# Second block's attention: VectorE scales head h-1 before it masks head h, instead of after

## The reference

```
h = rms_norm_2(x, g_pre_mix)
q, k, v = split_heads(h, w_qkv)              # 16 heads of 64
sc = q @ k.T / 8 + bias[head]                # causal by chunks of 64; 256 queries, 256 keys
p = softmax(sc)                              # exp(sc - max) / sum
m = merge_heads(p @ v) @ w_o
x = x + rms_norm_2(m, g_post_mix)
x = x + rms_norm_2(swiglu(rms_norm_2(x, g_pre_ffn), w_gate, w_up, w_down), g_post_ffn)
```

## Time and profile before

| | us |
|---|---|
| median of three runs | 775.57 (774.2 to 777.39) |
| the profiled execution | 774.49, of which the span of instructions 772.7 |
| TensorE busy in the span | 734.9 (95%) |
| VectorE, ScalarE busy | 418.9 (54%), 338.0 (44%) |
| second block's attention, first mask to last values | 488.4 to 571.3 |
| granted TensorE clock, mean | 0.992 |

### The profile page before, as it was taken

One profiled execution on the slowest core, in us unless ns is written; L12 is line 12 of the kernel. 1 busy time (PEld: TensorE's weight loads), 2 busy tenths in 40 slices (PEclk: granted clock), 3 DMA queues, 4 the chain that ended last, 5 costly groups with the idle time before them and its releaser, 6 DMA issues.

```text
span 772.7 us, 12515 instructions
## 1 busy us (share of the span) xinstructions
PE 734.9 (95%) x5170; PEld 606.1 (78%) x5170; DVE 418.9 (54%) x738; ACT 338.0 (44%) x604; POOL 32.2 (4%) x64
## 2 busy tenths in 40 slices
PE   8999999999999999999877789999999999999997
PEld 8898888888788866666555559999878888888885
DVE  5667756667667421111010117666668777777675
ACT  5966565554444421111010128465656444344443
POOL 2700000000000000000000001000001000000001
PEclk9999999999999999999999999999999999999999
DMA  8953557347988999999999999953334454545101
GB/s 343 416 212 119 207 219 286 117 170 278 366 313 339 362 391 419 422 420 419 421 421 421 412 419 355 419 174 130 145 109 164 174 208 164 205 176 197 77 1 55
DMA packets 33018, 206.07 MB, mean 267 GB/s; under 512 B 3904, under 2 KB 4288, under 8 KB 11200
## 3 DMA queue, kind: packets, MB, share of 16 engines
q1 hardware_dynamic: 32960, 205.25, 68.2%
HBM read 204.18 MB, written 1.05 MB: 266 GB/s over the span
## 4 chain that ended last, share of the span: by engine, by line
PE 77%; DMA 12%; ACT 3%; SPq 3%; DVE 3%; issue 1%; POOL 0%; DVEq 0%; POOLq 0%; ACTq 0%
PE ps L697 41%; PE ps L767 10%; PE ps L770 5%; PE ps L1096 5%; DMA big<-in_w_gate_e 3%; DMA ext<-in_w_up_e 3%; DMA X<-in_w_down_e 3%; PE ps L1020 2%; PE ps L1117 2%; SPq L504 2%; PE ps L1127 1%; DVE wl L1821 1%; DMA big<-in_rel_ext 1%; ACT wh L1406 1%; SPq L530 1%
## 5 line engine op out<-in xcount | busy, mean ns | idle before, releaser
L1821 DVE TENSOR_TENSOR wl<-raw,wh 128x1024 fp32r<-128x1024 f32 (+3 forms) x181 | 213.2, 1195 | 132.4 <-ACT wh L1406 131.2
L1406 ACT CAST wh<-raw 128x1024 fp32r<-128x1024 f32 (+3 forms) x181 | 181.8, 1024 | 71.5 <-PE ps L697 47.6
L697 PE MATMUL ps<-wh,fra 128*128 128x512 f32 (+3 forms) x636 | 179.2, 367 | 0.5 <-DVE gb L2030 0.5
L697 PEld LDWEIGHTS ps<-wh,fra 128*128 128x128 f32 x636 | 112.9, 189 | 18.2 <-issue 1.0
L697 PE MATMUL ps<-wl,fra 128*128 128x512 f32 (+3 forms) x318 | 115.1, 362 | 0.0
L767 PE MATMUL ps<-fra,wh 128*128 128x512 f32 x352 | 110.7, 396 | 0.7 <-DVE fra L1832 0.7
L770 PEld LDWEIGHTS ps<-fra,wl 128*128 128x128 f32 x352 | 66.1, 188 | 15.5
L697 PE MATMUL ps<-wh,frb 128*128 128x512 f32 x240 | 74.3, 391 | 0.0
L770 PE MATMUL ps<-fra,wl 128*128 128x256 f32 x352 | 69.2, 278 | 0.0
L697 PE MATMUL ps<-fra,wh 128*128 128x256 f32 x368 | 68.0, 286 | 0.1
L697 PEld LDWEIGHTS ps<-wl,fra 128*128 128x128 f32 x318 | 59.9, 188 | 9.0
(11 more groups left out here) (291 smaller groups left out, 1009.7 us busy)
## 6 DMA issues: line engine op xcount, KB each, us to landing
raw<-in_dense SPq DMA_DIRECT2D x79, 1024.0 KB, 5.4
ext<-in_w_down_e SPq DMA_DIRECT2D x20, 1024.0 KB, 18.3
raw<-in_w_gate_e SPq DMA_DIRECT2D x17, 1024.0 KB, 23.4
ext<-in_w_up_e SPq DMA_DIRECT2D x14, 1024.0 KB, 21.1
big<-in_w_up_e SPq DMA_DIRECT2D x8, 1024.0 KB, 18.1
big<-in_w_gate_e SPq DMA_DIRECT2D x7, 1024.0 KB, 27.0
raw<-in_dense SPq DMA_DIRECT2D x13, 512.0 KB, 5.7
raw<-in_w_up_e SPq DMA_DIRECT2D x6, 1024.0 KB, 21.0
```

What stands on the lines that cost most here:

```text
L697: t = e.matmul(o, a, w, start=first and n == 0, stop=final and n == 2, skip_group_check=not check)
L1406: e.copy(halves(q)[0], piece_view(q)).then_inc(*up("wh", q))
L1821: e.tensor_tensor(l, piece_view(q), h.bitcast(F), ALU.subtract).then_inc(*up("wl", q))
```

## The change

In `attention` of VectorE a flag `late` is added. Where it is set, `soften(step)` is called behind the reciprocal and scaling of head step-1 and not ahead of it. Only the second block's attention sets it.

```diff
-        def attention(name, heads, soften, norm, finish):
+        def attention(name, heads, soften, norm, finish, late=False):
             for step in range(heads + 3):
-                if step < heads:
+                if step < heads and not late:
                     soften(step)
                 if 0 <= step - 1 < heads:
                     h = step - 1
@@
                         t = e.tensor_scalar(part, part, r[:, i:i + 1], None, ALU.mult)
                     t.then_inc(*up("softened", name, h))
+                if step < heads and late:
+                    soften(step)
                 if step >= 3:
                     finish(step - 3)
                 yield
@@
-        for step, _ in enumerate(attention("r", 16, r_soften, causal_parts, r_finish)):
+        for step, _ in enumerate(attention("r", 16, r_soften, causal_parts, r_finish, True)):
```

## The result

| | before | after |
|---|---|---|
| median, 22 runs each (us) | 775.21 | 777.55 |
| ratio | | 1.0026, 95% interval 1.0020 to 1.0033 |
| profiled execution, its span | 774.49, 772.7 | 778.17, 776.4 |
| first mask to start of the last transposes | 568.56 - 488.41 = 80.15 | 572.22 - 489.87 = 82.35 |

The account below looks back on a forecast made before the run. TensorE, busy 734.9 of 772.7 us, was taken as the bound; lengthened rounds make it 2.1 us late, 774.49 + 2.1 = 776.6, and half of the median's 1.1 us offset gives 777.2; range 774.8 to 779.8.

Parts of the forecast that it names:

- The gap at 499 us: TensorE's transposes wait 0.8 us for VectorE's scaling at the attention's start; forecast not shortened, TensorE 0.1 us later.
- The round: VectorE and ScalarE's mask, exponential, cast and subtraction each step; scaling adds 0.66 us, making 4.44 us without extras.
- rival 2: Attention rounds cost more, the mask finding no overlap or a gap behind the scaling: +3.3 to +5.0 us; chance 0.18.
- the sum of 777.8: With the skill's no-overlap rule the scaling in each round takes 0.74 us: 776.6 + 1.2 = 777.8.
- (a) to (d): TensorE late at scores of steps 12 and 14, transposes of 16 and 17: 0.9, 1.2, 1.75, 2.1 us.
- the cover that was costed at nothing: Weight loads free places some 2 to 5 us later, costed nothing; subtractions end 2 us or more before use.
- The 1.1 us between the profiled execution and the median: The median shown, 775.57, lay 1.1 us above the profiled execution; half of it was taken, giving 777.2.
- Rival 1: Attention rounds have slack, TensorE sees only the earlier scaling: 773.7, or just 0.1 us later; -0.8 to +0.5, chance 0.20.
- the 24.2 us of ScalarE's waits: ScalarE's waits for TensorE's transposes in the attention, in 14 places, read as time to spare.
- 9.13 against 8.17 us: From step 10, two rounds against two TensorE steps; rounds fall behind by nearly 1 us every two steps.
- the 54% of VectorE: VectorE's busy share in the profile before, read beside TensorE's 734.9 of 772.7 us.

Follow-up runs that it names:

- step 2 alone: The changed kernel with the exchange made only at step 2, all other steps as before, against the kernel before: ratio 0.9994 (0.9985 to 1.0003).

## Why the prediction was right

- **The gap at 499 us doesn't close: right.** TensorE was expected there 0.1 us later, at 499.96; less the 1.46 us it comes at 501.41 - 1.46 = 499.95, and the wait went from 0.77 to 0.83. The earlier scaling of head 1 is real (step 2 alone: 0.27), and the mask of head 1 behind the scaling of head 0 takes it back.
- **The round grows by the scaling: right.** 0.66 us was taken for a scaling ahead of a mask, of which no row stood in the trace before; after, it is 495.02 - 494.37 = 0.65:

```profile
494.37 0.16 DVE L1877 RECIPROCAL rt<-rt 128x2 f32<-128x2 f32 x1
494.56 0.55 DVE L1880 TENSOR_SCALAR S<-S,rt 128x128 f32<-128x128 f32 x2
495.02 0.28 DVE L1901 CUSTOM_DVE_ANT_0 S<-ps,big 128x128 f32<-128x128 f32 x1
```

  The mask begins 0.09 us before the scaling ends, so rival 2 (no overlap, or a gap) falls. The prediction quoted the Trainium skill, "VectorE: DVE Perf Modes", section "The DRAIN you can't avoid", without its exception: it says that the next operation does not start until the pipeline of the one before has emptied, and adds that one that is not held starts earlier. The 0.09 us fit the exception and not the rule without it, and the sum of 777.8 left it out.
- **The four places (a) to (d): right, in place and size.** Waits of 0.85 (0.8 expected), 0.27 (0.3), 0.34 (0.5), and the last transposes start 82.35 us behind the first mask, where the sum gave 570.83 - 488.41 = 82.42. Late in all it is 1.02, 1.37, 1.85 and 2.20 us, where 0.9, 1.2, 1.75 and 2.1 were forecast; the forecast counted from the rows of the chain, which let a piece begin only where the one before ends, up to 0.16 us behind the timeline's start (568.72 against 568.56). Waits of TensorE for a low half, the cover that was costed at nothing, do not show in this stretch.
- **TensorE passes it on to the end: right as far as seen.** Stretch +2.2, ratio +2.0 (interval 1.6 to 2.6). The 1.1 us between the profiled execution and the median, of which I took half, is nothing that the runs explain: with 22 runs the median of before is 775.21, and 775.21 + 2.1 = 777.3, against 777.2 forecast and 777.55 measured. The ends of the range, 774.8 and 779.8, follow from no sum (rival 2 at its largest would be 777.2 + 2.9 = 780.1). That 0.5% is the least that can be told from no change was too coarse: the interval here is 0.13% wide.
- **Rival 1** fell by the chain: it took the 24.2 us of ScalarE's waits as a reserve for the whole attention. The reserve is what the lead allows at each step; behind step 10, with one piece a step, it was used up. The rule of the Trainium skill that led to it ("Perfetto Trace Analysis", "Optimization Strategy": make what the bound engine's gap waits for start sooner) agrees with the run of step 2 alone (0.77 to 0.27); in the change as a whole what the gap waits for does not start sooner (0.83), since the same exchange a step before delays that chain.

## What to carry to other kernels

When two engines wait for each other every step, an operation beside that round costs nothing as long as idle time covers it, and the same operation in it costs its length at every step once the round has used up its lead on the bound engine; look at which side of the hand-over it stands before exchanging neighbours. Add up the round from start to start and hold it against the bound engine's step in each part of the loop: here 9.13 against 8.17 us decided, not the 54% of VectorE. A single wait in the chain is not always made by the instruction ahead of it; follow its chain back, which ran here through a memory fill 12 us before and the load that this waited for.

## What the runs showed that I had not expected

Two scalings of 128x128 and 128x256 numbers took 0.34 us from start to start where they multiplied a constant table by a fixed factor and wrote to scratch, and 0.46 where they multiplied S in place by a factor for each row (495.27 - 494.81). A single one took 217 to 290 ns against 286 to 349. The difference is about the same for both sizes (means 287 - 220 = 67 and 348 - 286 = 62 ns), so it is not one for each number. Which of the differences (kind of factor, in place or not) does it was not tried.
